# A two-block transformer kernel on one core: narrower first weight tile, one transfer for x, and a new order of the low-part work around the first attention

## The reference

```python
h = x @ w_in                                  # (256,1024) @ (1024,648)
c_q, k, v, k_idx, w_idx = split(h, [256, 384, 512, 640])
c_q = rms_norm(c_q, g_cq)
q, q_idx = c_q @ w_uq, c_q @ w_iq             # 16 heads x 64, 8 index heads x 128
k_idx = layer_norm(k_idx, g_ik, b_ik)         # 128 columns; w_idx has 8
score = sum_h w_idx[h] * relu(q_idx[h] @ k_idx.T)    # causal
sel = top_k(score, 64)                        # keys each query may see
out = softmax(masked q @ k.T / 8) @ v @ w_o
```

## Time and profile before

| | |
|---|---|
| median of 3 runs | 1200.99 us (1200.72 to 1201.28) |
| the profiled execution | 1200.21 us, its span 1198.3 us |
| TensorE busy | 1105.0 us, 92% of the span |
| GpSimd busy | 818.6 us, 68% |
| ScalarE busy | 554.3 us, 46% |
| VectorE busy | 468.6 us, 39% |
| mean granted TensorE clock | 0.968 of full |

### The profile page before, as it was taken

One profiled execution on the slowest core, in us unless ns is written; L12 is line 12 of the kernel. 1 busy time (PEld: TensorE's weight loads), 2 busy tenths in 40 slices (PEclk: granted clock), 3 DMA queues, 4 the chain that ended last, 5 costly groups with the idle time before them and its releaser, 6 DMA issues.

```text
span 1198.3 us, 15747 instructions
## 1 busy us (share of the span) xinstructions
PE 1105.0 (92%) x6630; PEld 961.8 (80%) x6630; DVE 468.6 (39%) x826; ACT 554.3 (46%) x746; POOL 818.6 (68%) x297
## 2 busy tenths in 40 slices
PE   7969999999999756899999999999887998999997
PEld 7857878888899645688888889999886896788886
DVE  4595311139606899731111041721245535111102
ACT  6663454353354564344434335355643534544430
POOL 4550399879498576359988848886575273898880
PEclk9989999999999975899999999999998999999999
DMA  9201655555365400175555535554344144655540
GB/s 360 98 10 40 247 205 176 185 194 184 141 234 188 141 1 1 55 272 184 189 195 177 176 141 193 193 177 142 109 149 164 36 141 158 227 195 176 182 169 36
DMA packets 27733, 186.94 MB, mean 156 GB/s; under 512 B 3200, under 2 KB 3456, under 8 KB 6288
## 3 DMA queue, kind: packets, MB, share of 16 engines
q1 hardware_dynamic: 25472, 179.32, 42.7%
q10 hardware_dynamic: 2192, 6.62, 1.8%
HBM read 184.88 MB, written 1.05 MB: 155 GB/s over the span
## 4 chain that ended last, share of the span: by engine, by line
PE 81%; DVE 12%; POOL 3%; ACT 3%; issue 1%; DMA 1%; SPq 0%; DVEq 0%; ACTq 0%
PE ps L367 25%; PE ps L369 24%; PE ps L368 24%; POOL wl L351 3%; DVE arena L1535 2%; DVE arena L1536 1%; PE ps L1199 1%; DVE arena L840 1%; PE ps L1929 1%; ACT wh L347 1%; DVE arena L1550 1%; DMA stage<-in_tiles 1%; PE ps L1064 1%; DVE arena L818 1%; DVE arena L1544 1%
## 5 line engine op out<-in xcount | busy, mean ns | idle before, releaser
L351 POOL TENSOR_TENSOR wl<-stage,wh 128x2048 fp32r<-128x2048 f32 x166 | 764.7, 4631 | 298.8 <-ACT wh L347 298.5
L347 ACT ACTIVATE wh<-stage 128x2048 fp32r<-128x2048 f32 (+1 forms) x168 | 318.3, 1906 | 87.9 <-DMA stage<-in_tiles 87.2
L367 PE MATMUL ps<-wh,xh 128*128 128x512 f32 (+1 forms) x776 | 293.7, 379 | 20.3 <-POOL wl L351 7.0
L369 PE MATMUL ps<-wh,xl 128*128 128x512 f32 (+1 forms) x776 | 288.0, 371 | 0.0
L368 PE MATMUL ps<-wl,xh 128*128 128x512 f32 (+1 forms) x776 | 287.6, 371 | 0.0
L367 PE MATMUL ps<-xh,wh 128*128 128x256 f32 x644 | 184.1, 286 | 8.6 <-DVE xl L1999 4.1
L367 PEld LDWEIGHTS ps<-wh,xh 128*128 128x128 f32 x776 | 146.8, 189 | 49.7 <-POOL wl L351 5.7
L368 PE MATMUL ps<-xl,wh 128*128 128x256 f32 x644 | 182.8, 284 | 0.0
L369 PE MATMUL ps<-xh,wl 128*128 128x256 f32 x644 | 182.7, 284 | 0.0
L369 PEld LDWEIGHTS ps<-wh,xl 128*128 128x128 f32 x776 | 146.6, 189 | 25.5
L368 PEld LDWEIGHTS ps<-wl,xh 128*128 128x128 f32 x776 | 146.9, 189 | 24.1 <-issue 0.5
(11 more groups left out here) (348 smaller groups left out, 1143.2 us busy)
## 6 DMA issues: line engine op xcount, KB each, us to landing
stage<-in_tiles SPq DMA_DIRECT2D x167, 1024.0 KB, 4.9
arena<-in_ln_g ACTq DMA_DIRECT2D x4, 512.0 KB, 3.6
arena<-in_ln_b ACTq DMA_DIRECT2D x4, 512.0 KB, 5.2
arena<-in_x_t SPq DMA_DIRECT2D x2, 512.0 KB, 5.6
stage<-in_tiles SPq DMA_DIRECT2D x2, 512.0 KB, 7.3
x_res<-in_x SPq DMA_DIRECT2D x1, 1024.0 KB, 20.5
out<-x_res SPq DMA_DIRECT2D x4, 256.0 KB, 2.3
arena<-in_pre_mix_norm ACTq DMA_DIRECT2D x1, 512.0 KB, 6.7
```

The lines of the kernel that those rows point to most:

```text
L347: nc.scalar.activation(wh[:, ring(n), part], stage[:, ring(n), part], ACT.Copy).then_inc(hi_done, 1)
L351: nc.gpsimd.tensor_tensor(wl[:, ring(n), :], stage[:, ring(n), :], wh[:, ring(n), :].bitcast(F32), ALU.subtract).then_inc(lo_done, 1)
L367: mm(out_, lh, rh, start=start, stop=False, skip_group_check=skip)
L369: return mm(out_, ll, rh, start=False, stop=stop, skip_group_check=skip)
```

## The change

Tile 0 is packed to its 136 used columns per block of rows (8 x 136 = 1088 of 2048 columns; the rest zero and not loaded), it is loaded and converted in one piece, and the first matmuls have 136 columns instead of 256. x comes in one transfer. ScalarE issues the loads of positions and constants after its second conversion of x. ScalarE converts tiles 5, 6, 7, 8 and 9 earlier in its order, and GpSimd makes the low parts of tiles 7 and 8 before `dsa_pool`; those of tile 9 on wait until the last pair of the attention loop is normalised.

```diff
-    columns(w_att, 648 - 256, 256)
+    keys = w_att.reshape(KD, P, -1)[:, :, 512:648].transpose(1, 0, 2).reshape(P, -1)
+    tiles.append(np.concatenate([keys, np.zeros((P, TW - KD * IW), keys.dtype)], axis=1))
...
-                sp.dma_start(stage[:, 0, TW // 2:], A["tiles"][0, :, TW // 2:]).then_inc(stage_in[0], 16)
+                sp.dma_start(stage[:, 0, 0:KD * IW], A["tiles"][0, :, 0:KD * IW]).then_inc(stage_in[0], 16)
...
         def setup_dve(dve):
             for c in range(4):
                 x_lo(dve, c, x_raw)
-                if c == 1:
-                    first_low(dve, 0, first_hi.sem, 1)
-            first_low(dve, 1, hi_done, 1)
+            first_low(dve, 0)
...
             for c in range(4):
-                if c % 2 == 0:
-                    act.wait_ge(xt_in[c // 2], 16)
+                if c == 0:
+                    act.wait_ge(xt_in, 16)
                 nc.scalar.activation(two(xh, c), two(x_raw, c), ACT.Copy).then_inc(xh_done.sem, xh_done.up())
                 if c == 1:
-                    act.wait_ge(half_in, 16)
-                    nc.scalar.activation(wh[:, 0, 0:TW // 2], stage[:, 0, 0:TW // 2], ACT.Copy
-                    ).then_inc(first_hi.sem, first_hi.up())
+                    setup_loads(act)
...
             nc.scalar.activation(small[:, 4:6], small[:, 2:4], ACT.Exp, scale=-0.5).then_inc(rs_cq.sem, rs_cq.up())
             act.wait_ge(rs_cq.sem, rs_cq.now())
+            hi_until(act, 5)
...
             index_plain(0)
             index_plain(1)
             index_turned(0)
-            hi_until(act, 5)
+            hi_until(act, 6)
             index_turned(1)
-            hi_until(act, 6)
+            hi_until(act, 7)
...   (the relus)
-            hi_until(act, 7)
+            hi_until(act, 8)
...   (k, q, kd)
-            hi_until(act, 8)
+            hi_until(act, 9)
...
-            for k in range(2):
-                sp.dma_start(x_raw[:, 4 * k:4 * k + 4, :], A["x_t"][:, 4 * k:4 * k + 4, :]).then_inc(xt_in[k], 16)
-                if k == 0:
-                    sp.dma_start(stage[:, 0, 0:TW // 2], A["tiles"][0, :, 0:TW // 2]).then_inc(half_in, 16)
+            sp.dma_start(x_raw, A["x_t"]).then_inc(xt_in, 16)
...
             setup_pool(pool)
-            for n in range(2, 7):
+            for n in range(2, 9):
                 lo(pool, n)
             dsa_pool(pool)
...
-            until(7, t_ffn0 + 12)
+            pool.wait_ge(pn_ready.sem, HEADS // 2)
+            until(9, t_ffn0 + 12)
```

More of the change, by code:

```diff
@@ L38 @@
 MAGIC = 1.5 * 2.0 ** 23
+IW = ID + IH
 RING = 6
@@ L280, in build @@
         late_in = sem("late_in")
-        xt_in, half_in = [sem("xt_in0"), sem("xt_in1")], sem("half_in")
+        xt_in = sem("xt_in")
         stage_in = [sem(f"stage_in{s}") for s in range(RING)]
@@ L295, in build @@
         numbers, trig_done, reduced_t, trig_t_done = signals("numbers trig_done reduced_t trig_t_done")
-        first_hi, first_lo = signals("first_hi first_lo")
+        (first_lo,) = signals("first_lo")
         cqh_done, sq_done, ss_ps, rs_cq, iq_ps, iq_done, q_ps, q1_rot, q1_done, kr_done, kis_ready, k_rot = signals(
@@ L345, in hi @@
             act.wait_ge(stage_in[ring(n)], come[n])
-            part = slice(0 if n else TW // 2, TW)
+            part = slice(0, TW if n else KD * IW)
             nc.scalar.activation(wh[:, ring(n), part], stage[:, ring(n), part], ACT.Copy).then_inc(hi_done, 1)
@@ L373, in low_ready @@
             if n < 2:
-                pe.wait_ge(first_lo.sem, n + 2)
+                pe.wait_ge(first_lo.sem, n + 1)
             else:
@@ L490, in reduce_angles, with first_low @@
             return V.tensor_scalar(x, y, 3.1415925, -3.1415925, ALU.min, ALU.max)
[L492 to L495, removed]
+        def first_low(dve, n):
+            dve.wait_ge(hi_done, n + 1)
+            c = slice(0, TW if n else KD * IW)
             V.tensor_tensor(wl[:, n, c], stage[:, n, c], wh[:, n, c].bitcast(F32), ALU.subtract
@@ L513, in setup_dve @@
             reduce_angles(dve, ang24.rearrange("p c f -> p (c f)"), ps[:, 2, 0:96], ps[:, 2, 128:224], 48,
-                          lambda: first_low(dve, 2, hi_done, 2)).then_inc(reduced.sem, reduced.up())
+                          lambda: first_low(dve, 1)).then_inc(reduced.sem, reduced.up())
         def setup_dve2(dve):
@@ L644, in dsa_pe @@
                 for k in range(KD):
-                    if t == 0 and k % 4 == 0:
-                        pe.wait_ge(first_lo.sem, first_lo.due(pe))
+                    if t == 0 and k == 0:
+                        pe.wait_ge(first_lo.sem, 1)
                     if t == 0 and k % 2 == 0:
                         pe.wait_ge(x_ready.sem, x_ready.due(pe))
-                    o = k * 256
-                    last = mm3(ps[:, 1, t * T:(t + 1) * T], (xh[:, k, x], xl[:, k, x]),
-                               (wh[:, 0, o:o + 256], wl[:, 0, o:o + 256]), k == 0, k == KD - 1)
+                    o = k * IW
+                    last = mm3(ps[:, 1, t * T:t * T + IW], (xh[:, k, x], xl[:, k, x]),
+                               (wh[:, 0, o:o + IW], wl[:, 0, o:o + IW]), k == 0, k == KD - 1)
             last.then_inc(used, 1)
@@ L942, in dsa_dve @@
         def dsa_dve(dve):
-            ki = bank2(1)[:, :, 120:248]
+            ki = bank2(1)[:, :, 0:ID]
             dve.wait_ge(used, 1)
@@ L950, in dsa_dve @@
             last.then_inc(ki_var.sem, ki_var.up())
-            V.tensor_scalar(wi, bank2(1)[:, :, 248:256], float(IH ** -0.5 * ID ** -0.5), None, ALU.mult)
+            V.tensor_scalar(wi, bank2(1)[:, :, ID:IW], float(IH ** -0.5 * ID ** -0.5), None, ALU.mult)
             dve.wait_ge(ki_rstd.sem, ki_rstd.due(dve))
@@ L2099, in _ @@
         def _(act):
-            setup_loads(act)
             setup_x_act(act)
```

## The result

The changed kernel takes 1214.6 us in the median (4 executions, 1213.22 to 1215.72); the kernel before took 1201.13 beside it. The ratio is 1.0112 with a 95% interval of 1.0095 to 1.0130: slower by some 13.5 us, clear of the interval though under 2%. The forecast of 1206.6 had the sign and the deciding mechanism right; the measured time lies 2.1 us above the range. The profiled execution has a span of 1213.7 us, 15.4 more than before.

A forecast was written before the change was run, and what follows sets the result against it. TensorE, busy 92% of the span, was taken as the bound, so only early stalls on the chain count. Terms -0.3 + 11.7 + 2.1 - 7.9 = +5.6 us on the median 1201.0 gave 1206.6; range 1192 to 1212.5.

The forecast's parts named there:

- The diagonal matrices, +11.7: Before L691: VectorE's 16 L987 wait on GpSimd's low parts of tiles 5 to 7; TensorE starts 11.7 us later.
- first form of rival A: Diagonal matrices: VectorE keeps its access through its chain, TensorE only 3.1 us late, 1195.9 us; half of 0.22.
- The clock behind it, +2.1: After TensorE's wait for the diagonal matrices: 4.2 us at half clock lose 2.1 us.
- The attention loop, -7.9: Attention loop without GpSimd low parts: L828 and L840 unstalled, fourth mask at 73.15 instead of 81.03, 7.9 us gained.
- less than the 4.1 us after which it fell: Attention loop: TensorE idles only 3 us, under the 4.1 us after which its clock fell, so the fourth mask follows its own engine.
- The start, -0.3: First stage: TensorE starts tile 1 at 17.0 instead of 17.34, 0.3 us gained; bounds 1.0 gain and 4.5 loss.
- Rival B: Start: late constants let GpSimd's tile 2 low part block L496; tile 1 starts 5.2 us later, 1212.1 us; chance 0.13.
- the sign named for B: Start: the blocked start would show in the profile as an L496 of over 4 us.
- by the same 6.6 us: Start: constants issued at 6.5 would land 6.6 us later, as before, at 13.1.

The follow-up runs named there:

- e3: The kernel before with only the new order of ScalarE's conversions and GpSimd's low parts: 1207.0 us, ratio 1.0067.
- e6: The changed kernel with the identity copied once into PSUM and the 16 diagonal matrices made from there: 1201.8 us, ratio 1.0020 to the kernel before.
- e5: The changed kernel with GpSimd waiting for VectorE's low part of tile 1 before it begins tile 2's: 1211.5 us, ratio 1.0107 to the kernel before.
- e1: The changed kernel with ScalarE issuing the loads of positions and constants first again: 1205.9 us, ratio 1.0067 to the kernel before.
- e10: The kernel before with only the two-column signal copy in the last block reading PSUM instead of SBUF: 1195.8 us, ratio 0.9976.

## Why the prediction was wrong

Point by point, in the order of its sum:

- **The diagonal matrices, +11.7.** Right. From the start of the stretch (8.05 us later than before) to L687 (19.5 later) 11.45 us were lost, nearly in the pattern forecast: 5 through by the end of the gap (4 forecast), two that waited for one low part each, and 9 where GpSimd ran dry (10 forecast). e3 and e6 show the cause from both sides. The first form of rival A, a chain that keeps its access, did not occur.
- **The clock behind it, +2.1.** Right in kind; L687 and L693 together took 8.2 us instead of 5.5, 2.7 more.
- **The attention loop, -7.9.** L836 at 1.01 us as forecast, the fourth mask 8.0 us better against the loop's own start. But 0.7 went again at the fifth (99.47): TensorE waited 2.9 us, from 89.19 to 92.09, and its clock was at half from 93.3 to 96.7 although the wait was short; 7.3 in all. The step that failed here is "less than the 4.1 us after which it fell": the length of one wait, read off one case, did not foretell the next. e5 shows the same at 3.7 us.
- **The start, -0.3.** This is the term that failed, and by it the range was missed. Rival B, given 0.13, is what happened, but for the instruction that was blocked: it was the first small one behind the constants (L507, 3.70 us) and not the low part of tile 1, so the sign named for B, an L496 of over 4 us, did not appear (L497 took 2.29). x landed at 5.74 (5.6 forecast), the first stage began at 10.33 (10.8), and its 48 matmuls took 0.111 us each (0.13). The failed number is the landing of the constants: "by the same 6.6 us" became 9.4 us behind the queued tiles. The low part of tile 2 started at 14.83 instead of 15.6 to 16.2, before VectorE's chain. Tile 1 began at 23.03, 5.7 us later than before, where the rival had priced 5.2.
- **What rival B left out.** It priced the wait and not its clock: tile 1 ran at half clock from 23.0 to 28.5, and L867 behind it came 8.05 us late, so 2.4 more. By the same reasoning that gave the matrices' wait its 2.1 us, rival B should have been 1214.5, not 1212.1. It would have come out at the measured time, to the tenth by luck, since its own waits and the other terms were off by 0.3 to 0.6 us each.

Sum as measured in the trace: 8.05 + 11.45 + 2.7 - 7.3 = 14.9 of the 15.4 us between the spans. Against the forecast's terms the start is off by 8.35 us and the other three by 0.25, 0.6 and 0.6. The rest, 0.5, lies behind the first stage: the same small copies of the HGRN layer come 14.9 us late at 457 us of the kernel before and 15.3 late at 499, and one execution each says no more.

The late constants and the blocked access are separated by e5: tile 1 starts at 17.34 before, at 19.67 with the constants late but GpSimd held back (2.3 us), and at 23.03 with both (3.4 more). That the landing was slow because the constants were issued behind the tiles is supported by e1 (7.5 us from the first place, 9.4 from behind) but not isolated from their number of small pieces.

## What to carry to other kernels

Before work is moved on GpSimd, list VectorE's SBUF-to-SBUF instructions in the stretch it is moved to: each costs up to one whole GpSimd instruction, and an idle-looking gap of GpSimd may be the only place in which they run. An operand in PSUM takes such an instruction out of the contest. Price every new wait of TensorE with its clock as well, and a load that is moved behind others with more than its old time to landing.

## What the runs showed of the hardware that was not expected

- TensorE's granted clock went to half around waits of quite different lengths. In the loop of the changed kernel a wait of 2.9 us was followed by half clock about 1.2 us after work had begun again, for 3.4 us. In e5 it fell about 3 us into a wait of 3.7 and stayed at half until about 25.7, 6 us into tile 1. In the kernel before it fell about 4 us into a wait of 9.9 and stayed at half for 4.3 us of work.
- A copy of two columns, 0.17 us alone, takes 4.34 us when it meets GpSimd, and decides 5.5 us of the kernel's time. That this varies between executions of one program is inferred from the two groups of times and from their absence in e10; no kernel has a profile of both.
- An `fp32r` matmul with 136 moving columns takes 0.111 us from start to start against 0.12 for 256: narrowing by nearly half bought 7%. Other widths below 256 were not measured.
